# Grouping the three row transfers of an attention operand on one semaphore in an eight-core hybrid decoder layer

## The chip, the cores and the metric

The kernel runs on the 8 cores of one Trainium2 chip, as one program that every core executes on its own slice of the sequence; the cores don't talk to each other. The metric is the device time in microseconds of the slowest core.

## The reference, cut to what matters

One decoder layer over a sequence of 16384 tokens and a width of 2048. A pre-normed, modulated input is projected, then an attention branch and a short convolution branch are gated, merged and projected again.

```
h = rms_norm(x, g_pre) * (1 + scale) + shift          # scale, shift, gate from c @ w_ada + b_ada
q, k, v, z_attn, cb, cc, cx, z_conv, g_attn, g_conv = split(h @ w_in)
q, k = partial_rope(q), partial_rope(k)               # first 32 of 128 channels of a head
for g, (window, dilation) in enumerate(((128, 1), (512, 4), (2048, 16))):
    out[g], lse[g] = dilated_window_attention(q[g], k[g], v[g])   # 8 heads each, head size 128
o = sum(softmax_over_g(lse) * out)                    # 1024 wide
y_attn = (o * silu(z_attn)) @ w_attn_o
y_conv = (cb * causal_conv3(cc * cx) * silu(z_conv)) @ w_conv_o
y = (sigmoid(g_attn) * y_attn + sigmoid(g_conv) * y_conv) @ w_o
return x + gate * rms_norm(y, g_post)
```

Inside a dilation group every query block of 128 looks at its own and at the previous key block of its strided subsequence.

## The kernel before, in words

Each core owns 2048 tokens and recomputes keys and values of a halo of 2048 tokens before them. One big SBUF tile (`arena`) is cut into buffers by hand; the class `Sched` records all operations of the five engines as lists, and works out waits from the bytes that each one reads and writes. It keeps them in cells of 256 bytes along a partition. It doesn't look at partitions: `Buf.v` takes a partition range `p`, but the cells of a view are the same for any `p`. The lists are then replayed, one per engine, in the order in which they were recorded. So SyncE, which issues nearly all plain DMAs, works strictly in order: a DMA that waits holds up all that were recorded after it. Line 206 is the issue of every DMA, line 227 every wait, line 510 the matmuls of `feat` (result with channels on the partitions), 521 those of `tokm` (tokens on the partitions), 527 the PSUM copies on ScalarE (`act_copy`), 533 the two-operand VectorE operations.

Every DMA increments a completion semaphore by 16. `Sched.dma` takes them in turn, 12 for each of the queues `sp`, `pool` and `act`; a DMA first waits for the one that used its semaphore before (12 DMAs earlier on that queue).

The order of the work:
- Start (0 to some 200 us): SyncE loads 32 tiles of `wada` for the modulation, VectorE adds them up. GpSimd's queue brings one position tile, then 16 weight tiles (`wblk`), then position tiles for the rotary tables.
- Halo keys and values of the third group, then for the groups in the order 1, 0, 2 (dilation 4, 1, 16): values (`tokm`), keys, queries (`feat`). Values go through 3 small staging buffers (`vst2`), filled by ScalarE and stored to the DRAM tensor `vs` by SyncE (`store_v`); all stores of one half of the heads write the same cell, so each waits for the one before it to land. Keys and queries go through 3 larger ones (`kst`), stored to `ks` and `qs`.
- Attention of a group runs beside the projections of the next one, and the third group's beside the first convolution units. `own_tick` (or `tick`) is called once per projection matmul group; a quad of 4 query blocks takes three ticks: `step_a` (scores, L840, mask and maximum on VectorE, exponentials on ScalarE, L860), `step_b` (transposes, L870), `step_c` (times values, L884; copied by ScalarE, L888; stored to `os`). A head is 4 quads, so 12 ticks.
- `att_load(ui + 1)` is called in the tick with m == 1 of a head's second quad (b == 1), behind that quad pair's `os` store: it loads the next head's operands into the other of two buffer sets. The halo keys (`kh`; for the third group into `khn`, from which `att_perm`, L808, copies them in another order on ScalarE), then the queries (`qs`), then the keys (`ks`) each come through the helper `rows` in three transfers: partitions 0 to 16, 16 to 32 and 32 to 128, from different DRAM rows. The values (`vs`, 4 transfers for the first group, 1 for the others) and the halo values (`vh`) follow. The head's first `step_a` comes 8 ticks after its `att_load`.
- Then convolution, merge and output projection, which are dense matmuls.

`rows` passes, for each of its transfers, the view `dst.v((0, n), p=(p0, p1))` as written. As the three views have the same cells, the second transfer waits until the first has landed, and the third until the second has.

Of the kernel before, what the change touches and what calls it, by code (L numbers as in the profile page):

```python
# [25 lines left out]
class View:  # L26
    __slots__ = ("ap", "space", "lo", "hi")

    def __init__(self, ap, space, lo, hi):
        self.ap, self.space, self.lo, self.hi = ap, space, lo, hi  # L30
# [44 lines left out]
        return View(self.ap[tuple(key)], "sb", self.lo + lo * self.esz, self.lo + hi * self.esz)  # L75

class Sched:
    def __init__(self, nc, stack, sbuf_bytes, n_dma_sems=12):
        self.nc = nc
        self.ops = {e: [] for e in ENGS}  # L80
        self.sems = {}
        for e in ENGS:
            self.sems[e] = stack.enter_context(nc.semaphore("s_" + e))
        self.cnt = {e: 0 for e in ENGS}
        self.pending = {e: False for e in ENGS}
        self.known = {e: {} for e in ENGS}
        self.ndma = n_dma_sems
        self.dma_val = {}
        self.dma_rr = {}
        for q in ("sp", "pool", "act"):  # L90
            for i in range(n_dma_sems):
                self.sems[("d", q, i)] = stack.enter_context(nc.semaphore("s_dma_%s%d" % (q, i)))
                self.dma_val[(q, i)] = 0
            self.dma_rr[q] = 0
        ncell = (sbuf_bytes + CELL - 1) // CELL
        self.cw = {"sb": [None] * ncell, "ps": [None] * 8, "v": []}
        self.cr = {"sb": [dict() for _ in range(ncell)], "ps": [dict() for _ in range(8)], "v": []}
        self.arena = stack.enter_context(nc.sbuf_tensor("arena", [128, sbuf_bytes], U8))
        self.psum = [stack.enter_context(nc.psum_tensor("pb%d" % i, [128, 512], F32)) for i in range(8)]
        self.sbuf_bytes = sbuf_bytes  # L100
        self.rr = {}
# [89 lines left out]

    def dma(self, queue, out, in_, reads=(), writes=(), **kw):
        i = self.dma_rr[queue]
        self.dma_rr[queue] = (i + 1) % self.ndma
        waits = self._deps(queue, reads, writes)
        kn = self.known[queue]
        sk = ("d", queue, i)
        if self.dma_val[(queue, i)] > 0 and kn.get(sk, 0) < self.dma_val[(queue, i)]:
            kn[sk] = self.dma_val[(queue, i)]
            waits.append((sk, self.dma_val[(queue, i)]))  # L200
        self.dma_val[(queue, i)] += 16
        tok = (sk, self.dma_val[(queue, i)])
        self._record(tok, reads, writes)

        def fn(e, out=out, in_=in_, kw=kw):
            return e.dma_start(out=out, in_=in_, **kw)  # L206

        self.ops[queue].append((waits, fn, ("dma", sk)))
        return tok

    def wait_tokens(self, eng, toks):
# [92 lines left out]
def build_program():  # L304
    nc = bass.Bass("TRN2", target_bir_lowering=False)
# [20 lines left out]
    with ExitStack() as st:  # L326
        S = Sched(nc, st, SBUF_BYTES)
# [23 lines left out]
        class Region:  # L351
            def __init__(self, lo, size):
                self.p, self.end = lo, lo + size
# [181 lines left out]
        def sub(v, ap):  # L535
            return View(ap, v.space, v.lo, v.hi)
# [25 lines left out]
        def prep_tr(T, p, bank):  # L562
            pb = S.ps(bank, BF16)
            for q in range(2):
                kc = 2 * p + q
                for i in range(4):
                    xh_ = xh[(T % 2) * 4 + i]
                    o = q * 512 + i * 128
                    S.op("pe", lambda e, xh_=xh_, kc=kc, o=o: e.transpose(out=pb.ap[:, o:o + 128], in_=xh_.ap[:, kc * 128:(kc + 1) * 128],  # L569
                                                                        identity=identB.ap),  # L570
                         reads=[xh_.v((kc * 128, kc * 128 + 128)), identB.all()], writes=[pb], signal=(q == 1 and i == 3))
            return pb
# [122 lines left out]
        p0 = [prep_tr(0, p, p) for p in range(7)]  # L695
# [8 lines left out]
        def perm(g, T, dstb):  # L704
            if g == 0:
                return dstb.v((512 * T, 512 * T + 512)), (lambda ap: ap)
            if g == 1:
                v = dstb.v((512 * T, 512 * T + 512))
                return (sub(v, v.ap.rearrange("p (r j) -> p r j", r=4)), lambda ap: ap.rearrange("p (j r) -> p r j", r=4))
            v = dstb.all()  # L710
            return (sub(v, dstb.ap.rearrange("p (r i) -> p r i", r=16)[:, :, 32 * T:32 * T + 32]),
                    lambda ap: ap.rearrange("p (i r) -> p r i", r=16))
# [31 lines left out]
        for T in range(4):  # L744
# [3 lines left out]
            for b in range(8):  # L748
# [4 lines left out]
                if b < 2:  # L753
                    hold.append((pv, sb))
                    if b == 1:
                        rope(hold[0][0], hold[1][0], tab[0], tab[1], 0, 512, hold[0][1].all(), hold[1][1].all(), lambda ap: ap, rt1)
                        for x in range(2):
                            S.dma("sp", kh_d[2][128 * x:128 * x + 128, 512 * T:512 * T + 512], hold[x][1].ap,
                                  reads=[hold[x][1].all()], writes=[c_kh[2][x]])
# [17 lines left out]
        def att_load(ui):  # L777
            g, h = GROUPS[ui // 8], ui % 8
            B = ua[ui % 2]

            def rows(dst, src, cells, n):
                for (p0, p1, r) in ((0, 16, 16 * h), (16, 32, 128 + 16 * h), (32, 128, 256 + 96 * h)):
                    cl = [cells[b] for b in range(r // 128, (r + p1 - p0 - 1) // 128 + 1)]
                    S.dma("sp", dst.ap[p0:p1, 0:n], src[r:r + p1 - p0, :], reads=cl, writes=[dst.v((0, n), p=(p0, p1))])
            kh = khn if g == 2 else khs[ui % 2]
            rows(kh, kh_d[g], c_kh[g], HG[g])
            rows(B["q"], q_d[g], c_q[g], TOK)
            rows(B["kO"], k_d[g], c_k[g], TOK)
            cols = slice(128 * h, 128 * h + 128)
            vO = B["vO"]  # L790
            cv = c_v[g][h // 4]
            if g == 0:
                S.dma("sp", vO.ap, v_d[0][:, cols].rearrange("(n p) c -> p n c", p=128), reads=[cv], writes=[vO.all()])
                S.dma("sp", vhs[ui % 2].ap[:, 0, :], vh_d[0][:, cols], reads=[c_vh[0][h // 4]], writes=[vhs[ui % 2].v(0)])
            elif g == 1:
                for n in range(4):
                    S.dma("sp", vO.ap[:, 4 * n:4 * n + 4, :], v_d[1][512 * n:512 * n + 512, cols].rearrange("(p r) c -> p r c", r=4),
                          reads=[cv], writes=[vO.v((4 * n, 4 * n + 4))])
                S.dma("sp", vhs[ui % 2].ap, vh_d[1][:, cols].rearrange("(p r) c -> p r c", r=4), reads=[c_vh[1][h // 4]],
                      writes=[vhs[ui % 2].all()])  # L800
            else:
                S.dma("sp", vO.ap, v_d[2][:, cols].rearrange("(p r) c -> p r c", r=16), reads=[cv], writes=[vO.all()])
                S.dma("sp", B["vH"].ap, vh_d[2][:, cols].rearrange("(p r) c -> p r c", r=16), reads=[c_vh[2][h // 4]], writes=[B["vH"].all()])
# [198 lines left out]
        for gi, g in enumerate(GROUPS):  # L1002
# [17 lines left out]
            for base, dd, cells in ((B_K, k_d, c_k), (B_Q, q_d, c_q)):  # L1020
                for a in range(2):
                    u = next_unit(base + 8 * g + 4 * a)
                    for pr in range(2):
                        rot = a == 0 and pr == 0
                        if hn and base == B_K:
                            pvs = []
                            for x in range(2):
# [4 lines left out]
                                if g == 1:  # L1032
                                    v = sb.all()
                                    dst, f = sub(v, v.ap.rearrange("p (r j) -> p r j", r=4)), (lambda ap: ap.rearrange("p (j r) -> p r j", r=4))
                                else:
                                    dst, f = sb.v((0, hn)), (lambda ap: ap)
# [13 lines left out]
                        for T in range(4):  # L1050
                            pvs = []
                            for x in range(2):
# [3 lines left out]
                                dst, f = perm(g, T, sbs[x])  # L1056
# [174 lines left out]
        for hf in range(2):  # L1231
            pool = GEN
# [167 lines left out]
```

How the kernel before makes its waits and increments, by code:

```python
        def run(e, lst):  # L224
            for waits, fn, post in lst:
                for k, val in waits:
                    e.wait_ge(sems[k], val)
                if fn is None:
                    continue
                ins = fn(e)
                if post is None:
                    continue
                if post[0] == "inc":
                    ins.then_inc(sems[post[1]], 1)
                else:
                    ins.then_inc(sems[post[1]], 16)
```

## Time and profile before

| | us |
|---|---|
| median of 3 runs | 3795.14 (3790.37 to 3961.22) |
| the profiled execution | 3792.83 |
| its span on the slowest core, core 0 | 3791.3 |
| spans of all cores | 3759.7 to 3791.3 |
| TensorE busy on core 0 | 3511.4 (93%) |
| VectorE, ScalarE busy | 1263.3 (33%), 906.4 (24%) |

The profile follows one execution on the slowest core. "L206" is line 206 of the kernel; since all DMAs have that line, they are told apart by their tiles: `arena<-ks` is a load from the DRAM tensor ks into SBUF, `vs<-arena` a store. PE is TensorE's matmuls, PEld its weight loads, SPq is SyncE's sequencer, PEclk the TensorE clock that was granted as a share of the full one.

### The profile page before, as it was taken

Reading aid. Unit: us, or ns where it says so; the run is one execution under the profiler, and the core shown is the slowest. Engines: PE = TensorE matmul, PEld = TensorE weight load, DVE = VectorE, ACT = ScalarE, POOL = GpSimd, SP = SyncE. Lnnn points to the kernel's source line nnn. Section 1 sums busy time; section 2 is a strip of 40 time slices with the busy share of each in tenths; the row PEclk is TensorE's granted clock in tenths of the full one; section 3 lists DMA queues with packets and bytes.
Section 4 is the critical chain, followed back from the end, with each engine's and each line's share of the span. In section 5 each row is a group of like instructions: output and inputs, shape, how many; then the busy total and the mean of one; then the engine's idle time right before and its main releaser. Section 6 shows DMA issues by size and latency. Waiting matters only on the chain.

```text
span 3791.3 us, 50717 instructions; the slowest of 8 cores (3759.7 to 3791.3 us)
## 1 busy us (share of the span) xinstructions
PE 3511.4 (93%) x18459; PEld 1732.3 (46%) x18792; DVE 1263.3 (33%) x1835; ACT 906.4 (24%) x1962; POOL 204.4 (5%) x390
## 2 busy tenths in 40 slices
PE   1489899999899999998999999999999999999998
PEld 1244444444445444455555554444444444444443
DVE  5433125202434233434445451111222263111143
ACT  1155421123232222234444211011100011010233
POOL 0100000000000000000000000000000000000000
PEclk9689999999999988999999999999999999999999
DMA  9935447334454454466666674445644465444653
GB/s 319 233 124 156 135 111 222 81 93 111 109 125 117 100 113 98 118 140 135 128 126 133 128 152 78 74 77 84 104 75 77 78 145 98 77 78 75 132 197 136
DMA packets 264247, 463.77 MB, mean 122 GB/s; under 512 B 101313, under 2 KB 174401, under 8 KB 249281
## 3 DMA queue, kind: packets, MB, share of 16 engines
q0 software_dynamic: 55584, 191.16, 30.8%
q1 hardware_dynamic: 208418, 269.34, 23.4%
q8 instruction: 154, 2.52, 0.3%
q14 instruction: 91, 0.75, 0.1%
HBM read 557.32 MB, written 92.14 MB: 171 GB/s over the span
## 4 chain that ended last, share of the span: by engine, by line
PE 75%; DMA 12%; DVE 5%; issue 3%; ACT 2%; SPq 1%; DVEq 0%; POOL 0%; ACTq 0%; POOLq 0%
PE pb L510 56%; PE pb L521 16%; DMA arena<-ks 3%; DVE arena L533 2%; DMA arena<-qs 2%; DMA arena<-kh 2%; DMA arena<-wada 2%; DMA arena<-pos 2%; SPq L206 1%; DMA arena<-wblk 1%; PE pb L840 1%; PE pb L884 1%; DVE arena L667 1%; PE pb L870 1%; DMA vs<-arena 1%
## 5 line engine op out<-in xcount | busy, mean ns | idle before, releaser
L510 PE MATMUL pb<-arena 128*128 128x512 bf16 (+1 forms) x11791 | 2535.0, 372 | 46.8 <-ACT arena L527 28.7
L510 PEld LDWEIGHTS pb<-arena 128*128 128x128 bf16 x12032 | 1166.2, 98 | 1315.1 <-issue 119.5
L521 PE MATMUL pb<-arena 128*128 128x512 bf16 x3652 | 838.8, 384 | 22.2 <-ACT arena L527 16.7
L533 DVE TENSOR_TENSOR arena<-pb,arena 128x512 f32<-128x512 f32 (+2 forms) x398 | 257.0, 661 | 1066.1 <-PE pb L510 383.8
L521 PEld LDWEIGHTS pb<-arena 128*128 128x128 bf16 x3744 | 365.3, 99 | 442.4 <-issue 45.8
L533 DVE TENSOR_TENSOR arena<-arena 128x512 bf16<-128x512 f32 (+3 forms) x422 | 302.1, 750 | 263.7 <-ACT arena L1127 214.3
L527 ACT CAST arena<-pb 128x512 bf16<-128x512 f32 (+1 forms) x318 | 182.0, 577 | 799.9 <-PE pb L510 394.0
L206 POOL DMA_DIRECT2D arena<-wblk x344 | 181.8, 533 | 3079.4 <-PE pb L510 1513.0
L860 ACT ACTIVATE arena<-arena 128x256 bf16<-128x256 f32 x384 | 190.3, 497 | 346.3 <-DVE arena L853 311.9
L849 DVE TENSOR_TENSOR arena<-pb,arena 128x512 f32<-128x512 f32 x192 | 131.6, 685 | 360.5 <-PE pb L840 349.1
L530 DVE COPY arena<-pb 128x1024 bf16<-128x1024 bf16 x96 | 66.2, 689 | 270.2 <-PE pb L870 270.2
L851 DVE TENSOR_REDUCE arena<-arena 128x2 f32<-128x512 f32 x192 | 132.1, 688 | 20.2 <-DVE arena L849 0.5
L1225 ACT ACTIVATE arena<-pb 128x512 f32<-128x512 f32 x64 | 38.2, 597 | 402.2 <-PE pb L510 402.2
L527 ACT COPY arena<-pb 128x512 f32<-128x512 f32 (+1 forms) x144 | 77.4, 538 | 231.1 <-PE pb L510 116.3
L1127 ACT ACTIVATE arena<-pb 128x512 f32<-128x512 f32 x64 | 38.2, 597 | 371.1 <-PE pb L510 371.0
L639 PE MATMUL pb<-arena 128*128 128x1 f32 x64 | 13.9, 352 | 121.8 <-DVE arena L667 121.8
L1217 ACT ACTIVATE arena<-pb 128x512 f32<-128x512 f32 x64 | 38.2, 598 | 279.5 <-PE pb L510 279.5
L840 PE MATMUL pb<-arena 128*128 128x128 bf16 x768 | 62.2, 225 | 26.4 <-DMA arena<-ks 14.6
L1115 DVE SCALAR_TENSOR_TENSOR arena<-arena 128x1024 f32<-128x1024 f32 x64 | 82.2, 1284 | 7.0 <-DVE arena L1115 0.5
L667 DVE SCALAR_TENSOR_TENSOR arena<-arena 128x2048 f32<-128x2048 f32 x30 | 70.5, 2351 | 23.5 <-DMA arena<-wada 21.9
L569 PE MATMUL pb<-arena 128*128 128x128 bf16 x512 | 42.4, 230 | 37.0 <-DVE arena L559 36.6
L840 PEld LDWEIGHTS pb<-arena 128*128 128x128 bf16 x768 | 52.7, 101 | 48.7 <-issue 32.3
(66 smaller groups left out, 1021.0 us busy)
## 6 DMA issues: line engine op xcount, KB each, us to landing
arena<-wblk POOLq DMA_DIRECT2D x344, 512.0 KB, 5.5
arena<-xin SPq DMA_DIRECT2D x48, 1024.0 KB, 7.6
arena<-wada SPq DMA_DIRECT2D x48, 1024.0 KB, 12.8
os<-arena SPq DMA_DIRECT2D x96, 256.0 KB, 3.3
arena<-os SPq DMA_DIRECT2D x96, 256.0 KB, 5.1
out<-arena SPq DMA_DIRECT2D x16, 1024.0 KB, 5.4
vs<-arena SPq DMA_DIRECT2D x96, 128.0 KB, 1.7
ks<-arena SPq DMA_DIRECT2D x24, 512.0 KB, 7.1
```

The lines of the kernel that those rows point to most:

```text
L206: return e.dma_start(out=out, in_=in_, **kw)
L510: S.op("pe", lambda e, kc=kc, r=r: e.matmul(pv.ap, lhsT=wb.ap[:, kc, :], rhs=r.ap, start=(kc == 0), stop=(kc == nk - 1)), reads=[wb.v(kc), ...
L521: S.op("pe", lambda e, kc=kc, lv=lv, rv=rv: e.matmul(pv.ap, lhsT=lv.ap, rhs=rv.ap, start=(kc == 0), stop=(kc == KC - 1)), reads=[lv, rv], ...
L527: S.op("act", lambda e: e.copy(out=dst.ap, in_=src.ap), reads=[src], writes=[dst])
L530: S.op("dve", lambda e: e.tensor_copy(out=dst.ap, in_=src.ap), reads=[src], writes=[dst])
L533: S.op("dve", lambda e: e.tensor_tensor(out=dst.ap, in0=a.ap, in1=b.ap, op=op), reads=[a, b] + list(extra), writes=[dst])
L667: S.op("dve", lambda e: e.scalar_tensor_tensor(out=a.ap, in0=w.ap, scalar=cf.ap[:, CF_C + kc:CF_C + kc + 1], in1=a.ap, op0=ALU.mult, op1=A ...
L840: S.op("pe", lambda e, pv=pv, qv=qv, kv=kv: e.matmul(pv.ap, lhsT=qv.ap, rhs=kv.ap, start=True, stop=True), reads=[qv, kv], writes=[pv], si ...
L849: S.op("dve", lambda e, pv=pv, sm=sm, m0=m0: e.tensor_tensor(out=sm.ap, in0=pv.ap, in1=msk.ap[:, m0:m0 + 512], op=ALU.add), reads=[pv, msk ...
L851: S.op("dve", lambda e, sm=sm, mo=mo: e.tensor_reduce(out=mo, in_=sm.ap.rearrange("p (t k) -> p t k", t=2), axis=mybir.AxisListType.X, op= ...
L860: S.op("act", lambda e, sm=sm, pr=pr, dv=dv, t4=t4: e.activation(out=pr.ap, in_=sm.ap, func=AF.Exp, scale=scale_qk, bias=nm.ap[:, t4:t4 + ...
L1115: S.op("dve", lambda e, x=x: e.scalar_tensor_tensor(out=ubuf.ap, in0=pbuf.ap[:, x:x + 1024], scalar=cf.ap[:, cw + x:cw + x + 1], in1=ubuf. ...
```

## The change

`Sched` gets a separate number of completion semaphores for each queue: 64 for `sp`, 16 for `pool`, 1 for `act` (which issues no DMA). A new method `dmas` issues several transfers as one group: the waits of the whole group stand ahead of its first transfer, all transfers increment one semaphore, by 16 each, and whoever needs any of them waits for the full sum. `rows` in `att_load` collects its three transfers and passes them to `dmas`, with the union of their source cells as read and the whole buffer as written. All else is as it was.

```diff
-    def __init__(self, nc, stack, sbuf_bytes, n_dma_sems=12):
+    def __init__(self, nc, stack, sbuf_bytes):
...
-        self.ndma = n_dma_sems
+        self.ndma = {"sp": 64, "pool": 16, "act": 1}
...
-            for i in range(n_dma_sems):
+            for i in range(self.ndma[q]):
...
+    def dmas(self, queue, pairs, reads=(), writes=()):
+        i = self.dma_rr[queue]
+        self.dma_rr[queue] = (i + 1) % self.ndma[queue]
+        waits = self._deps(queue, reads, writes)
+        kn = self.known[queue]
+        sk = ("d", queue, i)
+        if self.dma_val[(queue, i)] > 0 and kn.get(sk, 0) < self.dma_val[(queue, i)]:
+            kn[sk] = self.dma_val[(queue, i)]
+            waits.append((sk, self.dma_val[(queue, i)]))
+        self.dma_val[(queue, i)] += 16 * len(pairs)
+        tok = (sk, self.dma_val[(queue, i)])
+        self._record(tok, reads, writes)
+        for n, (out, in_) in enumerate(pairs):
+            def fn(e, out=out, in_=in_):
+                return e.dma_start(out=out, in_=in_)
+            self.ops[queue].append((waits if n == 0 else [], fn, ("dma", sk)))
+        return tok
...
             def rows(dst, src, cells, n):
+                rd, prs = set(), []
                 for (p0, p1, r) in ((0, 16, 16 * h), (16, 32, 128 + 16 * h), (32, 128, 256 + 96 * h)):
-                    cl = [cells[b] for b in range(r // 128, (r + p1 - p0 - 1) // 128 + 1)]
-                    S.dma("sp", dst.ap[p0:p1, 0:n], src[r:r + p1 - p0, :], reads=cl, writes=[dst.v((0, n), p=(p0, p1))])
+                    rd |= set(range(r // 128, (r + p1 - p0 - 1) // 128 + 1))
+                    prs.append((dst.ap[p0:p1, 0:n], src[r:r + p1 - p0, :]))
+                S.dmas("sp", prs, reads=[cells[b] for b in sorted(rd)], writes=[dst.v((0, n))])
```

## Rows read from the trace of the kernel before

**Rows 1.** Cores: span and mean granted clock.

```profile
core 0: 3791.3 us, clock 0.968
core 3: 3785.5 us, clock 0.973
```

**Rows 2.** The page's chain that ended last, by line.

```profile
PE pb L510 56%; PE pb L521 16%; DMA arena<-ks 3%; DVE arena L533 2%; DMA arena<-qs 2%; DMA arena<-kh 2%; DMA arena<-wada 2%; DMA arena<-pos 2%; SPq L206 1%; DMA arena<-wblk 1%; PE pb L840 1%; PE pb L884 1%; DVE arena L667 1%; PE pb L870 1%; DMA vs<-arena 1%
```

**Rows 3.** Waits of PE, core 0, whole span: us in total, times, longest.

```profile
PE pb L510 <- ACT arena L527: 28.7, 4, 15.2
PE pb L521 <- ACT arena L527: 16.7, 3, 6.3
PE pb L840 <- DMA arena<-ks: 14.6, 5, 8.3
PE pb L840 <- ACT arena L808: 11.8, 3, 4.0
```

**Rows 4.** Waits of SyncE's queue and one of ScalarE, core 0, 820 to 2400 us.

```profile
SPq L227 <- DMA arena<-ks: 156.7, 48, 9.5
SPq L227 <- DMA arena<-qs: 120.4, 46, 5.4
SPq L227 <- DMA arena<-kh: 115.0, 46, 9.3
ACT arena L527 <- DMA vs<-arena: 108.3, 18, 22.6
```

**Rows 5.** Timeline of SP, one load of a head: start, us, what.

```profile
956.34 5.85 SPq L206 DMA_DIRECT2D arena<-kh  x3
962.35 6.17 SPq L206 DMA_DIRECT2D arena<-qs  x3
968.56 11.86 SPq L206 DMA_DIRECT2D arena<-ks  x3
980.51 3.09 SPq L206 DMA_DIRECT2D arena<-vs  x4
983.64 2.77 SPq L206 DMA_DIRECT2D arena<-vh  x1
986.56 5.48 SPq L206 DMA_DIRECT2D vs<-arena  x3
```

**Rows 6.** Timeline of PE: idle time before an instruction and its releaser.

```profile
990.69 1.86 PE L510 MATMUL pb<-arena 128*128 128x512 bf16 x4 [15.20 <-ACT arena L527]
1362.76 1.86 PE L521 MATMUL pb<-arena 128*128 128x512 bf16 x4 [6.29 <-ACT arena L527]
1741.73 0.91 PE L840 MATMUL pb<-arena 128*128 128x128 bf16 x7 [8.27 <-DMA arena<-ks]
```

**Rows 7.** Issues on line 206: ns min/median/max, first and last start.

```profile
L206 SPq DMA_DIRECT2D arena<-ks x72: 302/304/1774, 817.8 to 2048.0; - x72
```

**Rows 8.** The chain in order of time: start, us, what.

```profile
906.15 3.45 PE pb L521 x16
931.76 5.50 PE pb L521 x16
```

**Rows 9.** Stretches of core 0: length, PE, PEld, DVE, ACT, POOL busy, PEclk, DMA share, GB/s.

```profile
1369.00:1531.00 162.00, 160.58 (x807) 77.61 (x822) 58.45 (x94) 41.21 (x123) 5.29 (x10) 0.81 0.47 102
2400.00:3000.00 600.00, 597.04 (x2725) 271.05 (x2780) 136.43 (x187) 56.57 (x95) 48.03 (x91) 1.00 0.49 82
106.00:143.00 37.00, 7.97 (x40) 7.68 (x40) 18.39 (x14) 1.40 (x3) 8.46 (x16) 0.50 1.02 264
```

**Rows 10.** The chain at the start: start, us, what.

```profile
143.54 42.99 DMA arena<-pos
```

**Rows 11.** Waits of PE, core 3, 820 to 2070 us.

```profile
PE pb L510 <- ACT arena L527: 30.5, 4, 15.4
PE pb L840 <- DMA arena<-ks: 25.4, 8, 8.0
PE pb L521 <- ACT arena L527: 17.6, 3, 7.5
```

More of the change, by code:

```diff
@@ L193, in dma @@
         i = self.dma_rr[queue]
-        self.dma_rr[queue] = (i + 1) % self.ndma
+        self.dma_rr[queue] = (i + 1) % self.ndma[queue]
         waits = self._deps(queue, reads, writes)
@@ L208, in dma @@
         self.ops[queue].append((waits, fn, ("dma", sk)))
+        return tok
+    def dmas(self, queue, pairs, reads=(), writes=()):
+        i = self.dma_rr[queue]
+        self.dma_rr[queue] = (i + 1) % self.ndma[queue]
+        waits = self._deps(queue, reads, writes)
[11 more added lines that the diff above has]
+            self.ops[queue].append((waits if n == 0 else [], fn, ("dma", sk)))
         return tok
```

## The prediction

> **What bounds the kernel now.** I read the cores first: core 0 is slowest, core 3 is 6 us shorter at a somewhat higher mean clock [rows 1]. Then the page's chain that ended last: most of it is matmuls, but behind them come the loads from ks, qs and kh with 3, 2 and 2% of the span [rows 2]. The chain walks back through SyncE's queue, so these shares (7% would be 265 us) are not time to be won; that is only what TensorE itself stands still or runs slowly. So the third view is the waits of PE [rows 3]: for ScalarE's copies L527 28.7 and 16.7 us in 7 stalls, for ks 14.6 us in 5, for the copy L808 11.8 us in 3. All lie between 900 and 2070 us, where attention runs beside other work. Who holds up L527 is seen one step on: ScalarE waited 108.3 us for stores of V to land [rows 4], as its three staging buffers were full. Those stores are late because they are queued on SyncE behind a head's load, and there SyncE waited 156.7, 120.4 and 115.0 us for landings of ks, qs and kh [rows 4]. One load shows it whole: kh, qs and ks take 5.85, 6.17 and 11.86 us with three transfers each, the values 3.09 and 2.77 us; SyncE is held from 956.3 to 986.4, the V store follows at 986.56, and PE, idle since 975.5, goes on at 990.69 after 15.20 us [rows 5, 6]. In the third group's heads, beside the convolution, no V store is queued; there the last ks transfer itself is late: PE waited 8.27 us for it before 1741.73 [rows 6].
>
> **The change, part by part.**
>
> *The waits inside a group* go. 24 heads times 3 operands times 2 waits are 144, of which 140 are in the three rows of 48, 46 and 46: 392.1 us, 2.8 us each [rows 4]. A load then costs SyncE its issues: 9 row issues of 0.30 us at the median [rows 7], with the gaps between them 3.4 us, and the values as before, 3.09 + 2.77 = 5.9 us [rows 5]. That is 9.3 us in place of 30.1 us for the load shown. The vh issue of 2.77 us is far above 0.30: an issue can be held back while much is outstanding, and now the values are issued with all the rows still under way. So the bounds of a load are 9.3 us, and 30 us if nothing overlaps and all of its time is bytes. I take 10 to 14 us, with the next V store landed 13 to 18 us after the load's start, because the first two transfers of each group carry an eighth of its rows each and still took 2 us and more: that was the time to a landing and not the bytes.
>
> *Does that clear PE's stalls?* The load at 956.34 led to a stall 19.2 us after its start (990.69 less 15.20), and the one with the earliest onset, whose load began at 1339.9, after 16.6 us (1362.76 less 6.29) [rows 6]. A V store landed at 13 to 18 us comes ahead of nearly all onsets, so the waits for L527 go: 28.7 + 16.7 = 45.4 us. The ks waits go too, 14.6 us: the last rows of ks are issued some 3.4 us after a load's start instead of 20, and the wait that ended at 1741.73 arose 27 us after its load's start. The three waits for L808 stay, 11.8 us: ScalarE reached that copy late behind its own exponentials, with no idle time before it; earlier keys don't help. Removed: 60.0 us; bounds 0 (all of a load's time is bytes) and 60.0.
>
> *The clock behind each stall.* 16 matmuls take 3.45 us undisturbed and 5.50 us right after a stall, at 931.76 [rows 8]: 2.05 us lost, as the granted clock was at its lower level, 1.2 in place of 2.4 GHz, when PE began again. Bounds are 0 and 11 stalls x 2.05 = 23 us (7 for L527 and the 4 larger ones for ks). Since some of the 11 are short, I take 1.6 us each: 18 us.
>
> *What is late next.* A few loads will meet a run of weight transfers and let a V store through late: 2 us (0 to 20). Otherwise PE is back to back, as between 2400 and 3000 us [rows 9].
>
> *64 semaphores on sp.* A DMA waits for the one 12 places earlier. By the landings in the trace no such wait on SyncE ended last, so lifting them gives 0; a few more wait instructions of 0.02 us lie under the matmuls. -1 to +1 us.
>
> *16 semaphores on pool.* Here the limit did bind: at the start the last four weight tiles and a position tile were each issued as an earlier tile landed, that one at 143.54, and it took 42.99 us to land at 186.5 [rows 10]; VectorE and then PE wait for it. Now they are issued at once. But the 16 DMA engines were busy throughout (share 1.02 [rows 9]), and the position tile stays behind the same 16 weight tiles. The bytes decide: 0; bounds +5 (weights crowd the last wada loads) and -5 us.
>
> *The sum.* 3791.3 - 60.0 - 18 + 2 = 3715.3 us of span. The profiled execution took 1.5 us more than its span, so 3716.8; it lay 2.3 us under the median of the runs shown. Predicted: 3717 us, 2.1% under 3795.
>
> **The rivals.**
>
> *The 0.81 stretch does not come again.* On core 0 (and 1, but no other) the granted clock was 0.81 of full from 1369 to 1531 us [rows 9]; 0.19 of 162 us is 30 us. Nothing in the program sets these two cores apart. Without it the slowest is a core like 3: 3785.5 - (30.5 + 25.4 + 17.6) - some 24 for the clock, + 2 + 1.5: 3692 us [rows 1, 11]. For it: two cores of eight. Against: the runs at 3790 and 3795 suggest that some core has it each time.
>
> *The burst takes the wait's place.* A V store joins the queue behind some 1.8 MB issued at once. If it lands 22 us or more after the load's start, the stalls with the early onsets stay, about half of the L527 time. Price: 45.4 / 2 = 23 us and 6 of clock: 3746 us, up to 3760. For it: the vh issue of 2.77 us, and the 11.86 us of ks beside weights [rows 5]. Against: in the V phase the weights' queue is empty half the time, and then a group's three transfers needed little over 4 us in all.
>
> The Trainium skill (DMA: Bandwidth & Descriptors, "Queues, rings and completion order") says that an engine takes up a queue's descriptors in the order of their ring and takes turns between queues; by that rule a V store can't pass the burst, which is this rival's mechanism. No row shows a store behind such a burst. By the same page ("Rules for kernel authors") transfers to disjoint partition ranges share the engines and gain nothing side by side; were all of a load's time bytes, the sum would be 3793, unchanged.
>
> *Slower: the limited clock spreads.* The place is 900 to 2070 us, where PE would now run with hardly a pause on eight cores. If the 0.81 level held there and not for 162 us only, each 100 us of matmuls would take 23 us more: the 78 us of gain are eaten after a further 340 us of them, and for the remaining 940 us the time is 3717 + 216 = 3933 us. Against it: 600 us at 99.5% busy ran at a clock of 1.00 [rows 9].
>
> The Trainium skill (TensorE: Matmul & The Clock Gate, on the peak-current limiter) says that dense matmuls on three cores of a die bring the whole die to 13/16 while they last. By that rule the long dense stretch of before would have had it already; rows 9 speak against it, at least as a rule for every dense load.
>
> *It doesn't do what it says.* Had the V stores waited for something else (each also waits for the one before it), the time would stay within 5 us of 3793. Against: the V store's place at 986.56, right behind the load [rows 5].
>
> **How the numbers follow.** Forecast (stalls go, the 0.81 stretch stays) 0.46; without that stretch 0.21; burst 0.25; clock that spreads 0.04, half of it slower by over 2%; no effect 0.04. The range, 3688 to 3755, holds the first two and most of the third. About 2% is what a measurement of this kernel can tell from no change, so "faster" begins at 3719, just above the forecast: three in five of the forecast (0.28), nearly all of the second (0.20), 0.03 of the third make 0.51. Slower is 0.02; the rest, 0.47, is within 2%.
>
> **What would show it.** In the profile after: SyncE's waits for kh, qs and ks near zero; a load of 9 to 14 us; no PE wait for L527 over 2 us between 900 and 1660; no L840 wait for ks; three L840 waits of 3.9 us for L808 as before; 16 matmuls at 3.45 us throughout. The burst would show as V stores that take over 10 us to land, with L527 waits behind them; the clock rival as PEclk under 0.95 where PE isn't idle; a wrong step on pool as another landing than 186 us for the position tile. A time over 3755 would say that the loads' bytes, and not the waits between them, held the V stores.

## The result and the profile after

| | before | after |
|---|---|---|
| runs, us | 3790.4, 3795.1 | 3693.8, 3695.1, 3700.0 |
| profiled execution, us | 3792.8 | 3693.8 |
| spans of the 8 cores, us | 3759.7 to 3791.3 | 3675.7 to 3692.3 |

The ratio is 0.9746, with a 95% interval of 0.9717 to 0.9774: 2.5% faster, some 97 us. All times here and below leave out executions in which one die ran at a lower clock than the other. The forecast was 3717, the range 3688 to 3755.

The cores of the kernel after, beside [rows 1]:

```profile
core 0: 3684.1 us, clock 0.984
core 3: 3687.1 us, clock 0.983
core 5: 3692.3 us, clock 0.983
```

Core 5 is now slowest, but hardly: the cores lie within 17 us of each other, where before it was 32. Next the waits of PE on core 5, 820 to 2070 us (engine and line, us in total, times, longest), beside [rows 3]. The new method shifts line numbers: L510, L521, L527, L808 and L840 of before are L528, L539, L545, L828 and L860 here.

```profile
PE pb L860 <- ACT arena L828: 11.8, 3, 4.0
PE pb L1214 <- DVE arena L551: 4.3, 1, 4.3
PE pb L904 <- DVE arena L548: 3.8, 1, 3.8
```

No wait for the staging copies is left and none for ks, on this core and on the other seven. The three waits for the key permutation are as they were, the wait of L1214 was there before too (it has only moved into the window), and one stall of 3.8 us is new (2.0 to 2.3 us on cores 4, 6 and 7, none on cores 0 to 3). SyncE's queue and ScalarE, 820 to 2400 us, beside [rows 4]:

```profile
SPq L245 <- ACT arena L908: 552.8, 61, 16.4
SPq L245 <- DMA vs<-arena: 61.0, 30, 9.6
ACT arena L545 <- DMA vs<-arena: 25.6, 8, 8.0
```

kh, qs and ks are gone from the list of what SyncE waits for; it now mostly waits for ScalarE to have something to store. ScalarE's wait for V stores fell from 108.3 to 25.6 us, little enough for PE's four PSUM banks to cover. The load that answers to [rows 5]:

```profile
952.53 3.18 SPq L225 DMA_DIRECT2D arena<-kh  x3
955.86 1.23 SPq L225 DMA_DIRECT2D arena<-qs  x3
957.19 1.30 SPq L225 DMA_DIRECT2D arena<-ks  x3
958.64 2.62 SPq L206 DMA_DIRECT2D arena<-vs  x4
961.37 1.41 SPq L206 DMA_DIRECT2D arena<-vh  x1
962.98 13.98 SPq L206 DMA_DIRECT2D vs<-arena  x3
```

It holds SyncE for 10.3 us (952.53 to 962.78) and not 30.1. The last row is the rest of the trouble. Three V stores spread over 14 us, because each waits for the one before it, and those were slow. Three rows of the timeline tell what they met and what came of it (GpSimd starts four weight tiles; VectorE waits for a V store; PE waits for VectorE):

```profile
965.11 2.12 POOL L206 DMA_DIRECT2D arena<-wblk  x4 [64.19 <-PE pb L890]
...
981.60 0.29 DVE L551 TENSOR_TENSOR arena<-arena 128x128 bf16<-128x128 f32 x1 [4.69 <-DMA vs<-arena]
...
982.75 1.03 PE L904 MATMUL pb<-arena 128*128 128x128 bf16 x8 [3.81 <-DVE arena L548]
```

The second and third of these V stores, issued at 966.8 and 976.6, took 9.7 and 4.9 us to land, where a V store of the stretch before, from 930 to 952, took 1.7 to 2.5. It is the burst rival on a small scale, once per execution and not in every load, and with weight tiles under way beside the load. The stretches of core 5 (length, PE, PEld, DVE, ACT, POOL busy, PEclk, DMA share, GB/s):

```profile
820.00:1200.00 380.00, 376.19 (x2383) 196.54 (x2382) 141.90 (x245) 126.12 (x372) 12.38 (x24) 1.00 0.53 120
1200.00:1660.00 460.00, 460.00 (x2848) 240.56 (x2847) 178.02 (x291) 154.70 (x427) 17.73 (x34) 1.00 0.59 133
1660.00:2070.00 410.00, 393.89 (x2674) 233.63 (x2672) 200.59 (x341) 166.61 (x356) 25.86 (x49) 0.98 0.67 131
```

Between 1200 and 1660 us PE isn't idle at all, and the clock is granted in full: no core of this execution had a stretch at 0.81, which [rows 9] show on core 0 before.

### The profile page after: what moved, and what is told of

The parts are those of the page before. It is cut to its first block, busy times and chain, and to the rows that moved or that the text cites. A ratio compares the mean times of both kernels' runs of the same rounds, so it can differ in the third digit from the quotient of the medians.

```text
span 3692.3 us, 50906 instructions; the slowest of 8 cores (3675.7 to 3692.3 us)
## 1 busy us (share of the span) xinstructions
PE 3485.5 (94%) x18792; PEld 1720.0 (47%) x18792; DVE 1262.0 (34%) x1835; ACT 906.9 (25%) x1962; POOL 204.4 (6%) x390
## 4 chain that ended last, share of the span: by engine, by line
PE 86%; DVE 5%; DMA 4%; issue 2%; ACT 2%; SPq 0%; another core or an unknown queue 0%; DVEq 0%; ACTq 0%
PE pb L528 64%; PE pb L539 17%; DVE arena L551 3%; DMA arena<-wada 2%; DMA vs<-arena 1%; PE pb L860 1%; PE pb L904 1%; DVE arena L685 1%; PE pb L890 1%; DMA arena<-xin 1%; PE pb L587 1%; ACT arena L572 0%; PE pb L657 0%; ACT arena L828 0%; DVE arena L577 0%
## 5 line engine op out<-in xcount | busy, mean ns | idle before, releaser
L528 PE MATMUL pb<-arena 128*128 128x512 bf16 (+1 forms) x12032 | 2520.8, 369 | 6.5 <-DVE arena L551 3.6
L528 PEld LDWEIGHTS pb<-arena 128*128 128x128 bf16 x12032 | 1158.7, 98 | 1266.4 <-issue 17.9
L539 PE MATMUL pb<-arena 128*128 128x512 bf16 x3744 | 837.2, 382 | 0.0
L539 PEld LDWEIGHTS pb<-arena 128*128 128x128 bf16 x3744 | 363.4, 98 | 419.3 <-issue 11.0
L545 ACT CAST arena<-pb 128x512 bf16<-128x512 f32 (+1 forms) x318 | 182.1, 576 | 683.8 <-PE pb L528 402.1
L545 ACT COPY arena<-pb 128x512 f32<-128x512 f32 (+1 forms) x144 | 77.4, 538 | 229.5 <-PE pb L528 115.9
L657 PE MATMUL pb<-arena 128*128 128x1 f32 x64 | 13.9, 352 | 124.5 <-DVE arena L685 124.5
L587 PE MATMUL pb<-arena 128*128 128x128 bf16 x512 | 42.4, 230 | 37.0 <-DVE arena L577 36.5
L572 ACT ACTIVATE arena<-arena 128x2048 bf16<-128x2048 f32 x32 | 61.3, 1914 | 47.7 <-DMA arena<-xin 47.7
L657 PEld LDWEIGHTS pb<-arena 128*128 128x128 f32 x64 | 13.8, 332 | 124.6 <-issue 124.6
```

What stands on the lines that cost most here:

```text
L528: S.op("pe", lambda e, kc=kc, r=r: e.matmul(pv.ap, lhsT=wb.ap[:, kc, :], rhs=r.ap, start=(kc == 0), stop=(kc == nk - 1)), reads=[wb.v(kc), ...
L539: S.op("pe", lambda e, kc=kc, lv=lv, rv=rv: e.matmul(pv.ap, lhsT=lv.ap, rhs=rv.ap, start=(kc == 0), stop=(kc == KC - 1)), reads=[lv, rv], ...
L545: S.op("act", lambda e: e.copy(out=dst.ap, in_=src.ap), reads=[src], writes=[dst])
```

## The experiments

**1. Which part of the change.** One kernel has the grouping with 12 semaphores on each queue, the other only the semaphores.

```diff
# e1_group12
-        self.ndma = {"sp": 64, "pool": 16, "act": 1}
+        self.ndma = {"sp": 12, "pool": 12, "act": 12}
```

> The grouping of the three row transfers alone, with 12 completion semaphores on each queue as in the kernel before. Theory (the waits inside a group are all of the gain; the semaphores are worth nothing): the time of the changed kernel, about 3695 us, and the same waits of PE, 11.8 us for the copy behind attention's key permutation and none over 5 us for V's staging copies. Rival (more semaphores let transfers be issued earlier and carry part of the gain): at least 10 us slower than 3695.

```diff
# e2_sems_only, against the kernel before
-        self.ndma = n_dma_sems
+        self.ndma = {"sp": 64, "pool": 16, "act": 1}
```

> 64, 16 and 1 semaphores alone, the three row transfers issued one by one as before. Theory: the time of the kernel before, about 3790 us; only the weight tiles at the start are issued earlier, and the position tile still lands at about 186 us. Rival (semaphores carry part of the gain): 10 us or more under 3790.

Grouping alone: 3695.5, 3697.4 and 3699.7 us, ratio to before 0.9723 (0.9704 to 0.9743). Semaphores alone: ratio 0.9997 (0.9982 to 1.0011). All of the gain is the grouping. The semaphores do move the issues at the start, as its timeline of POOL on core 4 shows:

```profile
124.21 1.59 POOL L206 DMA_DIRECT2D arena<-wblk  x3 [5.25 <-DVE arena L667]
125.77 0.56 POOL L206 DMA_DIRECT2D arena<-pos  x1
```

The position tile is issued at 125.8 and no longer at 143.5, and it takes 64.6 us to land in place of 43.0: at 190.4 us, where before it was 186.5, in a start that as a whole ran some 2 us later on this core. Over the eight cores it lands at 185.8 to 189.8 us before and at 189.1 to 192.0 in e2. With the grouping it is the other way round: 189.4 to 193.5 with the late issue (e1), 186.6 to 191.0 with the early one (after). So an issue some 20 us earlier has no effect of one sign; that the bytes ahead of it decide fits this, but no run takes them away.

**2. How much hold costs how much.** Three kernels put back some waits of a load.

```diff
# e3_wait_in_ks: as below for ks alone; e4_wait_in_kh_qs: for kh and qs
+                if src is k_d[g]:
+                    for pr in prs:
+                        S.dmas("sp", [pr], reads=[cells[b] for b in sorted(rd)], writes=[dst.v((0, n))])
+                    return
                 S.dmas("sp", prs, reads=[cells[b] for b in sorted(rd)], writes=[dst.v((0, n))])
# e5_wait_between: groups whole, but each group waits for the one before
+            last = []
             def rows(dst, src, cells, n):
+                S.wait_tokens("sp", last)
...
+                last.append(S.dmas("sp", prs, ...))
...
             rows(B["kO"], k_d[g], c_k[g], TOK)
+            S.wait_tokens("sp", last)
```

> The changed kernel, with the waits put back inside the group of ks alone (2 of the 6 waits of a load). Theory (PE stalls when SyncE is held longer than the staging buffers cover, some 17 to 20 us): a load holds SyncE for about 18 us, near the onset, so a part of the 95 us comes back, not a third in proportion: 3700 to 3725 us, with the ks waits of the third group's heads still gone or under 5 us. Rival (each removed wait is worth the same): a third of 95, 3727 us or more.

> The changed kernel, with the waits put back inside the groups of kh and qs (4 of the 6 waits of a load), ks grouped. Theory (threshold): SyncE is held some 20 us per load, so V's stores are late in the same loads as before but by less: 3710 to 3745 us. Rival (each wait is worth the same): two thirds of 95, 3758 us or more.

> The changed kernel, groups as they are, but the group of qs is issued only when kh has landed, that of ks when qs has, and the values when ks has: 3 waits per load in place of none, and no burst of all operands. Theory (what counts is how long SyncE is held, up to some 17 us it is free): a load holds SyncE about 17 us, so 0 to 15 us slower than the changed kernel, 3695 to 3710 us, and the few late V stores are no earlier. Rival (the burst of all operands costs something of its own, by crowding out stores and weights): as fast as the changed kernel or faster, with the one 3.8 us stall near 980 us gone.

The waits of PE on core 0, 820 to 2070 us, of these three in turn:

```profile
PE pb L528 <- ACT arena L545: 10.8, 2, 9.8
PE pb L539 <- ACT arena L545: 0.6, 1, 0.6
```

```profile
PE pb L528 <- ACT arena L545: 17.5, 4, 12.0
PE pb L539 <- ACT arena L545: 5.4, 2, 2.9
PE pb L864 <- DMA arena<-ks: 1.1, 1, 1.1
```

```profile
PE pb L528 <- ACT arena L545: 15.4, 2, 10.6
PE pb L539 <- ACT arena L545: 4.6, 2, 2.3
```

Set beside the mean time for which a load held SyncE, over the loads 3 to 16 (from its first kh issue to the end of its vh issue; lowest and highest core):

| kernel | waits left per load | hold, us | PE's staging waits, us | time, us |
|---|---|---|---|---|
| after | 0 | 10.2 to 11.4 | 0 | 3694 to 3700 |
| e3, in ks | 2 | 15.2 to 15.8 | 11 to 16 | 3712 to 3714 |
| e5, between groups | 3 | 18.2 to 19.6 | 20 to 26 | 3726, 3739 |
| e4, in kh and qs | 4 | 18.3 to 20.4 | 23 to 29 | 3733 to 3736 |
| before | 6 | 23.2 to 24.3 | 43 to 51 | 3785 to 3826 |

The hold orders them all, but so does the number of waits left, and neither is proportional to the time. Beside the mean of the kernel after (3696), the 4 waits of e4 take back 39 of some 100 us and the 2 waits of e3 17, where equal shares would be 67 and 33.

In e3 the hold isn't even what stalls PE most. Its one large stall (8.2 to 13.5 us on the eight cores, of 11 to 16 in all) lies behind a load that held SyncE for only 12.7 to 13.9 us. The V store went out right behind that load, among or just after four weight tiles on GpSimd's queue, and took 13.6 to 17.6 us to land. So it was late by its landing and not by the hold; that the weight tiles made it slow is read from the times, and no run takes them away. Core 0 (weight tiles; V stores; ScalarE, which waited for the first of them; PE):

```profile
956.11 2.12 POOL L206 DMA_DIRECT2D arena<-wblk  x4 [64.18 <-PE pb L894]
957.43 16.30 SPq L206 DMA_DIRECT2D vs<-arena  x3
971.62 0.59 ACT L545 CAST arena<-pb 128x512 bf16<-128x512 f32 x1 [17.17 <-DMA vs<-arena]
972.35 3.15 PE L528 MATMUL pb<-arena 128*128 128x512 bf16 x7 [9.75 <-ACT arena L545]
```

In e5, and in e4 on seven of the eight cores, the large stall has the other cause: its V store took only 4.4 to 7.7 us to land but was issued 23 us or more after the load's start. In the kernel before it is the same: 30.2 us after the start on core 0, then 3.3 us to land. So two things make a V store late, the hold of the queue and a run of weight tiles just ahead of it.

For e5 I had put the hold at 17 us and the time at 3695 to 3710. Single loads reached 23 to 27 us, and the faster execution came out 16 us above that. The other one, 3739, holds an accident: on cores 4 and 5 the clock was at 0.81 in two stretches near the start, which cost them some 25 us each (core 4, columns as above):

```profile
152.40:190.00 37.60, 35.65 (x138) 14.75 (x136) 8.00 (x12) 10.10 (x14) 0.54 (x1) 0.81 1.03 192
210.50:311.40 100.90, 99.36 (x480) 46.06 (x479) 28.16 (x48) 43.19 (x63) 0.53 (x1) 0.81 0.47 118
```

The other six cores of that execution, on which the level came for at most 6 us at the very end, finished at 3709 to 3725 us, so 3726 is the time to set beside the rest. The rival of e5 fares worse: without the burst of all operands the stall of 2 to 4 us near 980 is gone (1.0 us is left on one core), but nothing is faster, as the longer hold costs more.

**3. The queue, or the bytes.** In the kernel before, with all transfers one by one, the stores of the three own projections go to GpSimd's queue.

```diff
# e9_stores_pool, against the kernel before: store_v, and the kh, ks and qs stores of the own projections
-            S.dma("sp", dd[row:row + 128, 512 * ch:512 * ch + 512], sb.ap,
+            S.dma("pool", dd[row:row + 128, 512 * ch:512 * ch + 512], sb.ap,
```

> The kernel before, with nothing grouped, but the stores of values, keys and queries of the three own projections are issued by GpSimd's queue and not by SyncE's. Theory (V's stores are late because they stand behind a load in SyncE's in-order queue): PE's waits for the staging copies (45 us) go although a load holds SyncE as long as before; the ks waits (15 to 25 us) and those for the key permutation (11.8 us) stay: 3725 to 3745 us. Rival (the bytes of a load on the shared 16 DMA engines hold the stores up): the staging waits stay, 3785 us or more.

3766 to 3786 us, ratio 0.9915 (0.9882 to 0.9948): slower than I expected. Core 5, 820 to 2070 us for PE and to 2400 for SyncE:

```profile
PE pb L840 <- DMA arena<-ks: 30.7, 10, 8.2
PE pb L840 <- ACT arena L808: 11.8, 3, 4.0
```

```profile
SPq L227 <- DMA arena<-ks: 143.2, 46, 7.5
SPq L227 <- DMA arena<-qs: 137.4, 46, 6.4
SPq L227 <- DMA arena<-kh: 125.8, 46, 9.6
```

The mechanism is confirmed: SyncE waits as long as before inside the loads and the DMA engines move the same bytes, yet not one staging wait is left. With the waits of before inside a load, its bytes don't hold the stores up; the place behind it does. What I missed is that ks waits grew to 31 us on this core (38 to 58 on cores 4, 6 and 7). In the kernel before, PE was stalled for staging while a load ran and so came to the next head's scores later; with those stalls gone it gets there sooner, finds a load of still 26 us unfinished, and part of the time is given back. I argue that from the places of the new waits, six of which lie in the first two groups; no run isolates it. The loads themselves also grew, from 23.2 to 24.3 us before to 25.5 to 27.2 here (loads 3 to 16, mean of a core), which makes ks later by itself; how much of the 31 us is due to which is open. The grouping removes both at once.

**4. Two mechanisms in two places.**

```diff
# e10_wait_g2 (e11_wait_g01: g != 2)
+                if g == 2:
+                    for pr in prs:
+                        S.dmas("sp", [pr], reads=[cells[b] for b in sorted(rd)], writes=[dst.v((0, n))])
+                    return
```

> The changed kernel, with the waits put back inside all three groups, but only for the eight heads of the third attention group, which run beside the convolution. Theory (two separate mechanisms: V stores behind a load in the first two groups, a late ks in the third): no wait for the staging copies, ks waits of 12 to 25 us and their clock back, 3715 to 3730 us. Rival (the last rows of ks would have come in time there anyway once the earlier stalls are gone): within 6 us of the changed kernel.

> The reverse: the waits put back for the sixteen heads of the first two attention groups, the third one's grouped. Theory: the 45 us of staging waits and some 15 us of half clock come back, ks waits beside the convolution stay away: 3760 to 3778 us, and the two parts add up to the whole change within 10 us. Rival (both stretches depend on each other): they don't add up.

Waits of PE on their slowest cores, e10 first (core 2), then e11 (core 7):

```profile
PE pb L864 <- DMA arena<-ks: 29.4, 6, 9.0
PE pb L864 <- ACT arena L832: 11.8, 3, 4.0
PE pb L908 <- DVE arena L548: 5.6, 1, 5.6
```

```profile
PE pb L528 <- ACT arena L545: 33.7, 4, 15.7
PE pb L539 <- ACT arena L545: 16.9, 3, 6.7
PE pb L864 <- DMA arena<-ks: 3.0, 2, 2.2
```

e10 took 3729 and 3740 us, the second 10 us above what I expected; e11 took 3767, 3767, 3770 and 3783, the last 5 us above; the kernel before took 3791 to 3801 beside them. Against the mean of the kernel after, ungrouping the third group costs 33 and 43 us, ungrouping the first two 70 to 87 us. The means add up to 113 us. The whole change is worth 99 us by the executions of before beside these two, and 97 to 112 by those beside the result and the other experiments. I had expected a match within 10 us; whether the rest is spread or time that both parts claim is open. The two places are clearly apart, though: e10 has no wait for a staging copy in the first two groups, and e11 has only 1 to 3 us of ks waits on any core. e10 shows one more thing: its cores end between 3692 and 3738 us with ks waits between 9 and 29 us. This stall differs from core to core by chance, and the slowest core sets the time.

**5. What is left.** In e6 the key permutation comes three ticks earlier; e8 also brings the second position tile ahead of the weights.

```diff
# e6_perm_early and e8_perm_pos
-                        elif b == 3:
+                        elif b == 2:
                             att_perm(ui + 1)
# e8_perm_pos also, after the first rotary table (and rope_tab without its own load for T == 1)
+                S.dma("pool", tabH[1][1].ap, pos_d[:, 512:1024], writes=[tabH[1][1].all()])
```

> The changed kernel, with the key permutation of the third group's next head moved three ticks ahead, from the fourth quad to the third, since its source now lands some 10 us after the load's start. Theory (those three 3.9 us stalls are ScalarE reaching the copy too late, plus some 2 us of half clock each): 12 to 18 us faster than the changed kernel, about 3680 us. Rival (the copy of 3.9 us delays exponentials wherever it stands): within 4 us of 3695.

> As the kernel with the earlier permutation, and the second position tile of the start is issued ahead of the 16 weight tiles instead of behind them. Theory (the 21 us stall of PE near 181 us waits for that tile, which stands behind the weights in its queue and is not helped by semaphores): 30 to 40 us faster than the changed kernel, 3655 to 3665 us. Rival (PE would then wait for the next thing that the weights hold up, the input rows): 12 to 20 us faster, as with the permutation alone.

e6: 3681.3, 3685.9 and 3686.3 us, ratio to before 0.968 (0.9644 to 0.9716), some 12 us under the changed kernel by the means, at the lower end of what I expected. Its waits of PE (core 2, 820 to 2070 us) no longer name the permutation:

```profile
PE pb L1214 <- DVE arena L551: 4.3, 1, 4.3
PE pb L904 <- DVE arena L548: 4.3, 1, 4.3
```

So the 11.8 us went. The half clock that I counted on top came back as well: between 820 and 2070 us the lower clock cost PE 7.9 us per core in the kernel after and 2.4 us here (means over eight cores; how it is counted is told below). It hardly shows in the time because PE stood idle 5 us longer per core before 820 us in this execution, 171 us against 166. e8: 3675.6 and 3682.5 us, ratio 0.9666 (0.962 to 0.9712), some 5 us more than e6 by the means and not apart from it by their intervals. Its start on core 3 shows why the 21 us stall did not go:

```profile
185.50 0.22 PE L587 MATMUL pb<-arena 128*128 128x128 bf16 x1 [1.81 <-DVE arena L577]
...
194.39 1.91 ACT L572 ACTIVATE arena<-arena 128x2048 bf16<-128x2048 f32 x1 [1.74 <-DMA arena<-xin]
...
199.86 0.37 PE L587 MATMUL pb<-arena 128*128 128x128 bf16 x2 [14.15 <-DVE arena L577]
```

It shrank from 21 to 14 us, and the next thing that lands with the 16 weight tiles, the input rows, took over: they were issued at 167.56 and landed at 194.3, beside the last weight tile at 194.1. The rival was right here.

## Why the prediction was right or wrong

*The waits inside a group* went, all of them, and a load takes 10 to 11 us on average against 10 to 14 taken. Right; e1 and e2 show that nothing else in the change matters.

*PE's stalls.* The staging and ks waits that core 0 had, 60.0 us, are gone on all eight cores, and the L808 waits stayed at 11.8, as said. e9 shows the reason given (the place in the queue), e10 and e11 the two places. The V store right behind a load landed 11 to 19 us after the load's start in five of the six such loads on cores 0 and 5, where 13 to 18 was taken; in the sixth it took 23 to 24 us, without a stall.

*The clock behind each stall* was put at 18 us, and the traces bear it out. A row from the trace of before, right behind the stall that ended at 931.76, shows PE at work for all of 4 us at a mean clock of 0.55 (columns as in rows 9):

```profile
932.00:936.00 4.00, 4.00 (x11) 1.41 (x10) 0.00 (x0) 3.15 (x11) 0.00 (x0) 0.55 0.51 157
```

Counting over 820 to 2070 us half of the time for which PE was at work at half clock gives 21.4 to 29.4 us per core before and 6.3 to 9.9 after, 17.9 us less on the mean of the eight cores and 15.4 less on core 0.

*What is late next*: 2 us taken, 0 to 3.8 us by core, with the mechanism named.

*Semaphores on sp and pool*: 0 each, right (e2). The position tile landed no earlier for its earlier issue, as said.

*The step that failed* is the base of the sum. I took the stretch at 0.81 on core 0 for a part of every execution, "some core has it each time", and so put its going at 0 us. It came on none of the profiled cores after, and in the other two executions of the kernel after no core's mean clock was under 0.982, where it had been 0.968 with the stretch. Core 0 itself ended at 3684.1 us, 107.2 under before and not the 76 of the sum: 60.0 of stalls, 15.4 of half clock, 29.9 of the 0.81 stretch, and 2 of the rest. Whether an execution has it is luck as far as these traces show. It is missing in e2, whose waits are those of before, and a like stretch is there in e5, without the waits inside a group, each time on two neighbouring cores at once.

The inference behind it was wrong too. e2, which is as slow as the kernel before, was profiled at 3793.1 us on core 4 with no such stretch, but with more of the stalls themselves:

```profile
PE pb L510 <- ACT arena L527: 30.6, 4, 14.9
PE pb L840 <- DMA arena<-ks: 22.6, 6, 7.6
PE pb L521 <- ACT arena L527: 15.8, 3, 7.4
```

That is 69.0 us on that core against the 60.0 us of core 0. PE also stood idle 10 us longer there before 820 us, and lost 46 us to half clock in the whole span against 39. The time is the highest of eight cores, and the stalls vary by core (ks waits of 12 to 27 us on the cores of one execution). A change that removes a varying stall also removes the spread, so it gains what the worst core has, not what the profiled one has. The rival "the 0.81 stretch does not come again" gave 3692 us, by way of core 3's stalls, and is what happened, 3 us from the 3695 measured. Core 3 fell by 98.4 us: its 73.5 us of stalls, and 21.7 of half clock where some 24 were taken. The rivals of the spreading clock (1.00 with PE never idle from 1200 to 1660 us) and of no effect are refuted. The burst did not take the wait's place (3.8 us at most), but a V store can be slow to land: in e3 it took 14 to 18 us beside weight tiles.

## What to carry to other kernels

On an in-order issuing engine a wait costs whoever is queued behind it, even where the waiting transfer itself is needed much later. Look for waits of a queue on transfers of its own; here dependency tracking that ignored partitions made three independent transfers into a chain. Price such a wait by how long the queue is held, and how long the transfer behind it then takes to land, against what the buffers cover. On several cores look at more than the profiled one: take out what only one execution has, such as a stretch at a lower clock, and then take the core with the most stalls.

## What the runs showed of the hardware that was not expected

The stretch at 0.81 of the clock: 161 us long, at the same time on cores 0 and 1 of the first profile of the kernel before and on no other core, and not under the denser load after. It came again in e5, at the same times on cores 4 and 5 and then on no other: 38 and 41 us long from 152 us on, and 101 us from 211 us on. Nothing run here explains it.

A V store lands in 1.7 us when little else is under way, and in 13.6 to 17.6 us when it is issued right behind a load of a head and beside four weight tiles (e3, all eight cores).

And earlier issue on a saturated queue bought nothing that shows: some 20 us earlier at the start, landing 3 us later in one pair of kernels and 3 us earlier in the other.
